# One-core decoder block: modulation columns made directly, the first product group taken by contraction halves, and several waits moved

## The reference, cut to what matters

```python
mod = silu(c) @ w_ada + b_ada            # nine sections: sh1, sc1, gt1, sh2, ...
x = x + 0.5*gt1 * swiglu(modulate(rmsnorm(x, g1), sh1, sc1), w1, w3, w2)   # feed-forward 1, d_ff 2816
x = x + gt2 * mixer(modulate(rmsnorm(x, g2), sh2, sc2))   # 4 heads of causal differential attention with rotary, and a gated short convolution
x = x + 0.5*gt3 * swiglu(modulate(rmsnorm(x, g3), sh3, sc3), ...)          # feed-forward 2
out = modulate(rmsnorm(x, g_final), shf, scf)
```

## Time and profile before

| | |
|---|---|
| median of 3 runs | 1878.57 us (1878.34 to 1880.4) |
| profiled execution: its own time | 1878.75 us |
| its span, first to last instruction | 1877.0 us |
| PE busy | 1820.2 us (97% of the span) |
| PEld busy | 1479.3 us (79%) |
| DVE busy | 1260.8 us (67%) |
| ACT busy | 772.9 us (41%) |
| POOL busy | 271.9 us (14%) |

### The profile page before, as it was taken

How to read it: one execution, slowest core, us unless ns; L and a number is a source line. 1 busy time by engine, 2 the same in 40 slices (tenths; PEclk the granted TensorE clock), 3 DMA queues, 4 the chain that set the end, 5 groups by cost and what they waited for, 6 DMA issues and landing times.

```text
span 1877.0 us, 23217 instructions
## 1 busy us (share of the span) xinstructions
PE 1820.2 (97%) x8394; PEld 1479.3 (79%) x8394; DVE 1260.8 (67%) x1952; ACT 772.9 (41%) x1392; POOL 271.9 (14%) x411
## 2 busy tenths in 40 slices
PE   6999999999999999999999999999999999999997
PEld 3878888888888877888877777787888888888885
DVE  5887777777586776444326668687767666576767
ACT  4643333333344554111125555563333333344445
POOL 2011211211210000000303330201111111111000
PEclk9999999999999999999999999999999999999998
DMA  8165565664775312111211110325454545477432
GB/s 321 58 228 208 199 227 196 227 216 169 270 215 157 99 62 79 45 45 46 68 35 44 46 34 1 135 91 202 164 190 174 214 156 175 160 261 218 129 96 90
DMA packets 100529, 269.77 MB, mean 144 GB/s; under 512 B 13120, under 2 KB 13504, under 8 KB 100288
## 3 DMA queue, kind: packets, MB, share of 16 engines
q1 hardware_dynamic: 62608, 146.30, 22.8%
q0 software_dynamic: 34304, 117.46, 18.4%
q10 hardware_dynamic: 3504, 4.53, 1.0%
HBM read 209.53 MB, written 54.53 MB: 141 GB/s over the span
## 4 chain that ended last, share of the span: by engine, by line
PE 86%; DVE 7%; ACT 3%; issue 1%; DMA 1%; POOL 1%; ACTq 1%; DVEq 0%; POOLq 0%
PE PS L1536 60%; PE PS L1532 25%; DVE NMax L1447 1%; DMA AdaFirst<-ada 1%; ACTq L877 1%; PE PS L1970 1%; DMA TmpA<-TmpA 1%; DVE X L1343 1%; DVE SqSum L1312 0%; DVE TmpA L1330 0%; DVE Ml L1246 0%; ACT PR L899 0%; DVE Wl L1041 0%; DVE Wl L1038 0%; DVE CT L1412 0%
## 5 line engine op out<-in xcount | busy, mean ns | idle before, releaser
L1536 PE MATMUL PS<-Bh,Wh 128*128 128x512 f32 x1120 | 437.3, 390 | 5.4 <-ACT T L659 5.4
L1536 PE MATMUL PS<-Bh,Wl 128*128 128x512 f32 x1120 | 435.9, 389 | 0.0
L1536 PE MATMUL PS<-Bl,Wh 128*128 128x512 f32 x1120 | 435.8, 389 | 0.0
L1536 PEld LDWEIGHTS PS<-Bh,Wh 128*128 128x128 f32 x1120 | 210.3, 188 | 51.0 <-issue 5.1
L1536 PEld LDWEIGHTS PS<-Bh,Wl 128*128 128x128 f32 x1120 | 210.2, 188 | 44.0
L1536 PEld LDWEIGHTS PS<-Bl,Wh 128*128 128x128 f32 x1120 | 210.3, 188 | 43.3
L1536 PE MATMUL PS<-Wh 128*128 128x512 f32 x616 | 240.4, 390 | 3.4 <-DVE Wl L1041 1.7
L1536 PE MATMUL PS<-Wh,Wl 128*128 128x512 f32 x616 | 239.7, 389 | 0.0
L1536 PE MATMUL PS<-Wl,Wh 128*128 128x512 f32 x616 | 239.7, 389 | 0.0
L1038 DVE TENSOR_TENSOR Wl<-RawB,Wh 128x512 fp32r<-128x512 f32 x154 | 106.6, 692 | 135.9 <-ACT Wh L634 134.8
L634 ACT ACTIVATE Wh<-RawB 128x512 fp32r<-128x512 f32 x154 | 97.3, 632 | 229.9 <-PE PS L1536 229.9
(11 more groups left out here) (195 smaller groups left out, 2891.5 us busy)
## 6 DMA issues: line engine op xcount, KB each, us to landing
Raw<-up_w SPq DMA_DIRECT2D x86, 512.0 KB, 5.4
Ada<-ada POOLq DMA_DIRECT2D x72, 512.0 KB, 4.1
g_dram<-T SPq DMA_DIRECT2D x88, 256.0 KB, 2.1
W2s<-down_w POOLq DMA_DIRECT2D x88, 256.0 KB, 4.4
s_dram<-W2s POOLq DMA_DIRECT2D x88, 256.0 KB, 2.6
GQ<-g_dram POOLq DMA_DIRECT2D x88, 256.0 KB, 3.5
RawB<-s_dram SPq DMA_DIRECT2D x88, 256.0 KB, 2.8
RawB<-down_w SPq DMA_DIRECT2D x66, 256.0 KB, 2.7
```

The source lines that it names most:

```text
L1536: return nc.tensor.matmul(out, lhs, rhs, start=first, stop=last, skip_group_check=True)
```

## The change

**Start.** The host lays out the first two sections of `w_ada` by column halves: `AdaFirst` now holds, for each of the 8 contraction tiles, the first 512 columns of sh1 beside the first 512 of sc1; `AdaSecond` holds the second halves. POOL loads 8 tiles of `AdaFirst`, then 8 of `AdaSecond`. PE makes the means directly from the squares (4 one-column matmuls for every tile, summed in PSUM) and DVE's additions go. `first_cols` makes the columns directly: 128x128 blocks of `AdaFirst` are stationary and one column of `CAct` moves, 8 matmuls for each of 8 tiles. `AdaRow` goes. The second halves are still summed by DVE, now 8 operations of 1024 columns, and turned by `late_cols` inside the plain group. `spin(13, 3)` becomes `spin(8, 3)`.

**Plain group of feed-forward 1.** Chunks come by contraction halves: k 0 to 3 of both token halves, then k 4 to 7. `chunk_at`, `chunk_no` and `b_lo_of` hold the numbering. The first difference operand (`t_add`, `t_hi`, `t_lo` with 0, 1) is made during the last chunks.

**Waits moved.** ACT takes the copies `up_evict` 8 and 9 ahead of later weight splits; ACT splits the last down weight at step `N_DOWN - 5`; DVE takes the last `up_evict` ahead of `down_lo`. The rotary's `exchange` is issued by SP between its loads instead of by ACT. `score(0, 0)` no longer waits for all copies of V, and the first head starts with two projection chunks. `spin` at a head's end goes from 6 and 5 to 3 and 3. `mean(4)` comes one output tile later, `root(4)`, `spread(4)` and the first chunk of feed-forward 2 earlier, `spin(10, 6)` becomes `spin(5, 6)`, and ACT loads the square-root table a block earlier. The last mean takes the sum of 7 squares and the eighth square by itself, with `spin(5, 4)` ahead and `spin(4, 4)` behind it.

```diff
@@ POOL: loads @@
-                pool.dma_start(AdaFirst[:, 2 * c:2 * c + 2, :], ada[2 * c:2 * c + 2].rearrange("k p d -> p k d"))\
-                    .then_inc(first_loaded[c], 16)
-                load_second(c, 0)
+            for k in range(KT):
+                pool.dma_start(AdaFirst[:, k, :], ada[k]).then_inc(first_loaded[k], 16)
+            for k in range(KT):
+                pool.dma_start(AdaSecond[:, k, :], ada[KT + k]).then_inc(second_loaded[k // 2], 16)
...
@@ PE: start @@
+            def first_cols(k):
+
+                pe.wait_ge(first_loaded[k], 16)
+                for c in range(KT):
+                    made = mm_open(PS[:, 5, c:c + 1], AdaFirst[:, k, blk(c)], CAct[:, k:k + 1],
+                                   k == 0 and c == 0, k == KT - 1)
+                if k == KT - 1:
+                    made.then_inc(cols_done, 1)
...
+            for h in range(NH):
+                for k in range(KT):
+                    pe.wait_ge(sq_done, KT * h + k + 1)
+                    for b in range(4):
+                        made = mm_open(PS[:, 4 if h else 6, b:b + 1], Sq[:, k % 2, blk(b)], Mean[:],
+                                       k == 0 and b == 0, k == KT - 1)
+                    made.then_inc(sq_used if k < KT - 1 else mean_done, 1)
+            pe.wait_ge(square_loaded, 16)
+            bcast(0)
             pe.wait_ge(c_act, 1)
-            pe.wait_ge(consts, 1)
-            mean(0)
             for k in range(KT):
-                pe.wait_ge(first_loaded[k // 2], 16)
-                for c in range(D // HALF):
-                    made = mm(PS[0:1, c, :], CAct[:, k:k + 1], AdaFirst[:, k, half(c)], k == 0, k == KT - 1)
-                made.then_inc(row_used, 1)
+                first_cols(k)
                 if k == 1:
...
                     bcast(1)
-            second_cols(0)
-            pe.wait_ge(row_done, 1)
-            for c in range(KT):
-                made = mm(PS[:, 4, c:c + 1], AdaRow[0:1, blk(c)], Ones[0:1, :], True, True)
-            made.then_inc(cols_done, 1)
-            spin(13, 3)
+            spin(8, 3)
             up(0)
...
@@ PE: plain group of feed-forward 1 @@
+                if ph == 0:
+                    for k in range(KH):
+                        for j in range(4):
+                            plain_tile(0, 0, k, j)
+                    for j in range(4):
+                        for k in range(KH):
+                            if j == 2 and k == KH // 2:
+                                late_cols()
+                            plain_tile(0, 1, k, j)
+                    for h in range(NH):
+                        for k in range(KH, KT):
+                            for j in range(4):
+                                plain_tile(0, h, k, j)
+                    return
...
@@ ACT: up @@
-                for o in (11, 12):
-                    prep_hi(ph, o)
+                prep_hi(ph, 11)
+                up_evict(ph, 8)
+                prep_hi(ph, 12)
                 for t in range(8, N_UP):
                     if t == 10:
+                        up_evict(ph, 9)
                         t_hi(ph, 3, 6)
...
@@ ACT: down @@
-                    if m + AHEAD_B < N_DOWN:
+                    if m + AHEAD_B < N_DOWN - 1:
                         down_hi(ph, m + AHEAD_B)
...
+                    if m == N_DOWN - 5:
+                        down_hi(ph, N_DOWN - 1)
...
@@ ACT, heads @@
-                    if rotated:
-                        exchange(j, 0, TmpA[:, 1, :])
-                    if rotated and j % 2:
+                    if nxt and i in steps and j % 2:
                         split_hi(nq + 2 + j // 2, job_done, J + j + 1)
...
@@ SP @@
+            for m in range(1, HEADS):
+                for j in range(4):
+                    exchange(m, j, 0, TmpA[:, 1, :])
+                    n = U_Q1 + 2 * m + 3 + j // 2
+                    if j % 2 and n < UNITS:
+                        load_units(n, n + 1)
...
@@ PE: heads, output tiles, end @@
+            pe.wait_ge(aevac, AEVAC["att"] - 2)
+            score(0, 0)
             pe.wait_ge(aevac, AEVAC["att"])
             pe.wait_ge(evac, EVAC["att"])
-            score(0, 0)
...
-                if t == KT + 1:
+                if t == KT + 2:
                     mean(4)
...
-            spin(10, 6)
+            spin(5, 6)
             up(1)
             down(1)
-            mean(7)
+            spin(5, 4)
+            pe.wait_ge(*sums_of(7, KT - 2))
+            for b in range(4):
+                mm_open(PS[:, 6, b:b + 1], SqSum[:, 1, blk(b)], Mean[:], b == 0, False)
+            pe.wait_ge(sq_done, 8 * KT)
+            for b in range(4):
+                made = mm_open(PS[:, 6, b:b + 1], Sq[:, 1, blk(b)], Mean[:], False, True)
+            made.then_inc(mean_done, 1)
+            spin(4, 4)
             bcast(7)
```

More of the change, by code:

```diff
@@ L480, in _, with load_units, exchange @@
             sp.dma_start(Rope[:], rope_d).then_inc(rope_loaded, 16)
-            for n in range(RING, UNITS):
-                sp.wait_ge(lo_done, n - RING + 1)
-                sp.dma_start(Mr[:, n % RING, :], units[n]).then_inc(raw_loaded[n % RING], 16)
+            def load_units(first, last):
+                for n in range(first, last):
+                    sp.wait_ge(lo_done, n - RING + 1)
+                    sp.dma_start(Mr[:, n % RING, :], units[n]).then_inc(raw_loaded[n % RING], 16)
+            def exchange(m, j, slot, to):
+                sp.wait_ge(rraw, m * 4 + j + 1)
+                if m:
+                    sp.wait_ge(rope_done, m * 4 + j)
+                elif j >= 2:
+                    sp.wait_ge(rope_done, j - 1)
+                for a in range(0, P, 32):
+                    sp.dma_start(to[a:a + 32, :], TmpA[a ^ 32:(a ^ 32) + 32, slot, :]).then_inc(shifted[j % 2], 16)
+            load_units(RING, U_Q0 + 6)
+            for j in range(4):
+                exchange(0, j, j % 2, TmpG[:, j % 2, :])
+                if j % 2:
+                    load_units(U_Q0 + 6 + j // 2, U_Q0 + 7 + j // 2)
+            load_units(U_Q0 + 8, U_Q1 + 5)
+            for m in range(1, HEADS):
[4 more added lines that the diff above has]
+                        load_units(n, n + 1)
             for u in range(2):
@@ L809, in square_first @@
                 act.wait_ge(x_loaded[4 * h + k // 2], 16)
[L810 to L814, removed]
-                nc.scalar.activation(out, X[:, h, k, :], ACT.Square).then_inc(sq_done, 1)
+                if k >= 2:
+                    act.wait_ge(sq_used, (KT - 1) * h + k - 1)
+                elif h and k:
+                    act.wait_ge(mean_done, 1)
+                elif h:
+                    act.wait_ge(sq_used, KT - 1)
+                nc.scalar.activation(Sq[:, k % 2, :], X[:, h, k, :], ACT.Square).then_inc(sq_done, 1)
             for k in range(KT):
@@ L823, in _ @@
             root(1)
-            act.wait_ge(row_used, KT)
-            nc.scalar.activation(AdaRow[0:1, :], flat(PS[0:1, 0:2, :]), ACT.Copy).then_inc(row_done, 1)
             for o in range(4):
@@ L872, in raw @@
                                      scale=DH ** -0.5 if j < 2 else 1.0).then_inc(rraw, 1)
-            def exchange(j, slot, to):
-                for a in range(0, P, 32):
-                    act.dma_start(to[a:a + 32, :], TmpA[a ^ 32:(a ^ 32) + 32, slot, :]).then_inc(shifted[j % 2], 16)
             for c in (1, 2):
@@ L966, in body @@
                         split_hi(U_WO + 1 + i, job_done, LAST_PROJECTION)
+                    if not nxt and i == QB - 2:
+                        nc.scalar.activation(LamS[:, 7:8], EpsC[:, 0:1], ACT.Sqrt)
             exps(0, 0)
@@ L1549, in ada_between, with plain_tile @@
                         ada_cols(ADA_IN[ph][y // KT])
-            def plain_group(ph):
+            def plain_tile(ph, h, k, j):
+                pe.wait_ge(b_lo, b_lo_of(ph, chunk_no(ph, h, k)))
+                which, kk = operand(h, k)
+                o = 4 * (k // KH) + j
+                bank = PLAIN_BANKS[h][j]
+                if h == 0 and k % KH == 0:
+                    pe.wait_ge(w_lo, N_FFN * ph + o + 1)
+                if k == 0:
+                    plain_free(ph, h, j)
+                w = blk(k % KH)
+                mm(PS[:, bank, :], Wh[:, o, w], Bh[which][:, kk, :], k == 0, False)
+                mm(PS[:, bank, :], Wh[:, o, w], Bl[which][:, kk, :], False, False)
+                made = mm(PS[:, bank, :], Wl[:, o, w], Bh[which][:, kk, :], False, k == KT - 1)
+                if k == KT - 1:
+                    made.then_inc(prod, 1)
+                elif h == 1 and k == KH - 1 and j == 3:
+                    made.then_inc(half_used, 1)
@@ new lines, in late_cols @@
+            def late_cols():
+                pe.wait_ge(ada_used, KT)
+                pe.wait_ge(nm_done, NH * KT)
+                for c in range(KT):
+                    made = mm(PS[:, 6, c:c + 1], AdaSum0[:, blk(c)], Ones[:], True, True)
+                made.then_inc(cols_done, 1)
```

(4 more changed lines are left out.)

261 lines of the change are left out of this document (112 added, 149 removed).

## The result

The changed kernel takes 1887.54 us (median of 5 runs, 1886.58 to 1888.43) beside 1879.3 us of the kernel before on the same chip: ratio 1.0043, 95% interval 1.0028 to 1.0057. It is slower by some 8 us, and the forecast was 1888.0. Its profiled execution has a span of 1885.7 us, before 1877.0.

A forecast was written before the change was run, and what follows sets the result against it. PE, busy 97% of the span, was taken to bound the kernel. Start +24.2 us and moved waits -14.8 sum to +9.4, on 1878.75 gives 1888 us; range 1875 to 1898, the likeliest case's own 1881 to 1897.

The forecast's parts named there:

- start and plain group: From the start through the plain group: one-column matmuls at 0.213 us each delay products, +24.2 us, bounds 21.5 and 27.
- first seven-product tiles, feed-forward 1: PE's 4.1 us wait for ACT's copies shrinks as copies move ahead: -1.5 us, ends 0 and -4.1.
- the same, feed-forward 2: First seven-product tiles of feed-forward 2: the 1.3 us wait goes, DVE being further ahead: -1.3 us, ends 0 and -1.3.
- heads: Heads: ACT issues no exchanges, -3.2 us; earlier first score and its two chunks, -1.4; together -4.6, ends -1 and -9.
- after the heads: Around mean 4: one more tile fills the wait and keeps the clock, five spins less: -4.0 us, ends -1.5 and -5.
- The clock rises early: Rival at the start: back-to-back one-column matmuls raise the clock, products begin at 46 us, total 1863 us; chance 0.15.
- midway: Rival at the start: broadcasts or the second run raise the clock, columns cost about 14 us, total 1876 us; chance 0.06.
- some 2.6 us of waiting stay: First seven-product tiles, feed-forward 1: of PE's 4.1 us wait for ACT's copies, some 2.6 us remains.
- the order by halves costs nothing: Plain group: chunks take 1.4 us against 2.8 us of PE work, so no cost if the second scale is ready.
- Late next is that third copy: First seven-product tiles: ACT's third copy, still behind the difference operand, is the next late item; some 2.6 us waiting stays.
- waits for ACT's copies halved: Sign that the forecast is right: PE's waits for ACT's copies, 4.1 us in the first seven-product tiles, fall by half.
- if the first chunk is there: After the heads: five spins less save half of 2.39 us, provided the first chunk, now earlier, is ready.

## Why the prediction was right

The forecast was 1888.0 and the median is 1887.5. The start, which decided the sign, was right by its working. The gains (-14.8 forecast, -14.4 measured) came out by errors that cancelled, and that part is luck. The terms, measured from the product starts:

| term | forecast | measured |
|---|---|---|
| start and plain group | +24.2 | +23.2 |
| first seven-product tiles, feed-forward 1 | -1.5 | +3.1 |
| the same, feed-forward 2 | -1.3 | +0.7 |
| last `up_evict`, both | -0.4 | -2.2 |
| end of the first down stage | -1.5 | -2.1, then -0.3 to the heads |
| heads | -4.6 | -10.2 |
| after the heads | -4.0 | -2.6 |
| end | -1.5 | -0.9 |
| sum | +9.4 | +8.8 |

- **Start: right, for the reason given.** Two stages of 27.3 us were forecast, and 27.3 and 27.0 stand in the timeline. The decisive step, that one-column pairs neither raise nor hold the clock through stages this long, is shown by the run with wide spins ahead alone: 0.50 from 12.2 us on, as in the earlier trace rows. The changed kernel's own trace has no record of the clock before 68.05 us; there the price tells it. "The clock rises early" and "midway" fell. The Trainium skill ("TensorE: Matmul & The Clock Gate", section "LDWEIGHTS (loading the stationary operand)") prices a load of 128 columns at some 107 ns, by which the two stages would have taken an estimated 27 us instead of 55. A pair here costs 119 ns at 1.00 (0.95 us for 8), which is near it, but 213 at 0.50, so at the low clock the measurement decides against it.
- The sizes inside: in this trace PE started at 7.0 and not 8.0, hand-overs cost nothing, and the clock was granted as the last spins ran, so no product ran at half pace: 21.5 instead of 24.1. Some of that is this trace's own: in five of the six other runs with this start PE began at 8.0 to 8.2 and the first product came 22.5 to 22.9 us later than before, and with the third copy ahead products ran 2.5 us at the low clock, where the forecast had some 2. The plain group took 1.7 us more where +0.1 stood: late columns 1.84 us, less the turn that went, and 0.83 us waiting for the low part of the last chunk, since VectorE makes eight sums between the chunks.
- **First seven-product tiles: the step "some 2.6 us of waiting stay" failed, and with it "the order by halves costs nothing".** "Late next is that third copy" was right: it comes at 130.26 us, 24.5 us later than the 105.78 of before, while PE was 23.2 later. But the waits gathered into one of 3.9 us, and behind it the clock fell, which the sum had at nothing: another 2.6 us here. Either part of the change does this without the other: the copies ahead with the old start (a wait of 3.7 us, 1.8 us lost), and the new start with the old copies (a wait of 3.6). Making parts of VectorE's chain earlier wins 3.8 and 4.2 us, so the chain sets the wait. The late columns are some of the delay (3.1 us of wait with them and the sums moved up); the order by halves was not undone alone, so its own share is not shown. The sign "waits for ACT's copies halved" did not come: 4.5 us beside 4.1.
- In feed-forward 2 the forecast had the wait of 1.3 us gone, since VectorE is further ahead there. A wait of 1.5 us stays, and with the copies in their old place these tiles take 0.7 us less.
- **Heads: the mechanism was right, the size not.** The exchanges give 6.3 where I took 3.2: 3.3 of it is idle time, as forecast, and 3.0 is shorter busy time of TensorE, a term that the sum did not have. The 15 spins, which the prediction left out too, give 1.3.
- The last `up_evict`, put at under 1 us in both stages, is 1.2 and 1.0: the whole gap ahead of the first down weight went.
- **After the heads**, the low clock behind mean 4 is gone, as forecast. The condition "if the first chunk is there" failed in part: PE waits 0.9 us for its low part, about what the five spins fewer saved.

## What to carry to other kernels

A wait is the end of a chain: moving its last link ahead can move the wait to the next operation, and may gather two short waits into a long one that costs the clock too. Starting the chain earlier is what shortened it here, from 3.1 and 3.7 us to 1.5. Count one-column matmuls by the clock that the work around them leaves, and look at that work before multiplying them. A sum that comes out right needs its terms checked against the trace: here two terms were wrong by some 5 us each, with opposite signs.

## What the runs showed that I had not expected

- In the run with 256 columns between the pairs the clock fell (0.50 from 14.3 us) with TensorE busy throughout; in the run with 512 it stayed (1.00 to 67.6 us).
- A single wait for copies or additions of 3.1, 3.6, 3.7, 3.9 and 4.3 us in the first seven-product tiles was followed by the low clock each time. Behind 1.5 us it was not, nor behind the two of the earlier trace rows with products between them.
- A short run of the kind did not always lose the clock. In the run with the old start and the earlier differences, PE issued the same 24 one-column matmuls and 26 spins from 36.3 to 42.5 us at a grant of 1.00, where before it fell at 39.84. The clock was granted from 20.56 us on (before, 22.76) and fell at 54.69, for 3.4 us; TensorE had by then waited 1.15 us for a column sum and made its 8 one-column matmuls.
- So that run's first product came at 42.76 us, 4.0 earlier than in the run with the old start alone (46.72). By the end of the plain group 1.6 us of it were left. The start of a single trace can mislead by some 2 us.
